# One transformer-and-retrieval encoder kernel on Trainium2: the routing table's transposes moved half a piece earlier, more table rounding on ScalarE, one key-score copy moved

## The reference

```python
q = (xc @ w_query).reshape(-1, PEER_HEADS, 2, PEER_HALF)
s1 = jnp.einsum('thd,hkd->thk', q[:, :, 0], sub_keys[:, 0]).astype(jnp.float32)
s2 = jnp.einsum('thd,hkd->thk', q[:, :, 1], sub_keys[:, 1]).astype(jnp.float32)
v1, i1 = lax.top_k(s1, PEER_TOPK)
v2, i2 = lax.top_k(s2, PEER_TOPK)
cand = (v1[..., :, None] + v2[..., None, :]).reshape(...)      # 256 sums per head
cidx = (i1[..., :, None] * PEER_N_KEYS + i2[..., None, :]).reshape(...)
sv, pos = lax.top_k(cand, PEER_TOPK)
eidx = jnp.take_along_axis(cidx, pos, axis=-1)
gate = jax.nn.softmax(sv, axis=-1)
u = u_tab[eidx]
act = jax.nn.gelu(jnp.einsum('thkd,td->thk', u, xc), approximate=False)
w = gate.astype(act.dtype) * act
return jnp.einsum('thk,thkd->td', w, v_tab[eidx])
```

## Time and profile before

| | us |
|---|---|
| median of 3 runs | 3840.44 (3839.34 to 3841.6) |
| the profiled execution | 3837.75 |
| its span in the trace | 3835.9 |
| PE busy | 3751.9 (98%) |
| ACT busy | 799.2 (21%) |
| POOL busy | 2339.5 (61%) |
| DVE busy | 2280.8 (59%) |

### The profile page before, as it was taken

How to read it: one execution, slowest core, us unless ns; L and a number is a source line. 1 busy time by engine, 2 the same in 40 slices (tenths; PEclk the granted TensorE clock), 3 DMA queues, 4 the chain that set the end, 5 groups by cost and what they waited for, 6 DMA issues and landing times.

```text
span 3835.9 us, 52905 instructions
## 1 busy us (share of the span) xinstructions
PE 3751.9 (98%) x18640; PEld 3098.6 (81%) x18640; DVE 2280.8 (59%) x3843; ACT 799.2 (21%) x1357; POOL 2339.5 (61%) x1204
## 2 busy tenths in 40 slices
PE   7999999999999999999999999999999999999998
PEld 6778887888888888888877788878888888888886
DVE  8545998994777422222385469989757773222224
ACT  1551112451111101111015411134411111101011
POOL 6445576336777666666664555853377776666664
PEclk9999999999999999999999999999999999999999
DMA  3122234887555333333222222358865553333331
GB/s 143 66 72 99 97 143 157 244 246 251 190 187 206 132 121 117 125 120 120 88 94 73 77 98 102 136 178 245 248 234 207 186 191 119 129 120 120 120 116 70
DMA packets 230075, 554.96 MB, mean 145 GB/s; under 512 B 10048, under 2 KB 141376, under 8 KB 181440
## 3 DMA queue, kind: packets, MB, share of 16 engines
q1 hardware_dynamic: 47680, 335.57, 24.6%
q10 hardware_dynamic: 182272, 217.75, 17.1%
HBM read 446.32 MB, written 106.95 MB: 144 GB/s over the span
## 4 chain that ended last, share of the span: by engine, by line
PE 91%; DVE 4%; POOL 2%; issue 2%; ACT 1%; DMA 0%; ACTq 0%; POOLq 0%; SPq 0%; DVEq 0%
PE bank L1161 28%; PE bank L1162 28%; PE bank L1163 28%; PE bank L1489 2%; PE bank L1490 2%; POOL part_l L405 1%; POOL part_h L416 1%; PE bank L1287 1%; PE bank L1447 1%; PE bank L1275 1%; DVE q_turn L844 0%; PE bank L1266 0%; PE bank L1267 0%; DVE tables L816 0%; DVE X L775 0%
## 5 line engine op out<-in xcount | busy, mean ns | idle before, releaser
L405 POOL TENSOR_TENSOR part_l<-landing,part_h 128x1024 fp32r<-128x1024 f32 x632 | 1636.5, 2592 | 372.5 <-ACT part_h L670 325.0
L416 POOL TENSOR_SCALAR part_h<-landing 128x1024 fp32r<-128x1024 f32 x564 | 706.8, 1253 | 1078.1 <-PE bank L1163 830.5
L1161 PE MATMUL bank<-XTh,part_h 128*128 128x512 f32 (+1 forms) x2688 | 1050.9, 391 | 18.3 <-POOL part_l L405 8.2
L1162 PE MATMUL bank<-XTl,part_h 128*128 128x512 f32 (+1 forms) x2688 | 1036.5, 386 | 0.0
L1163 PE MATMUL bank<-XTh,part_l 128*128 128x512 f32 (+1 forms) x2688 | 1036.5, 386 | 0.0
L1161 PE MATMUL bank<-part_h,Wh 128*128 128x512 f32 x2048 | 796.9, 389 | 0.9 <-POOL part_l L405 0.9
L1162 PE MATMUL bank<-part_l,Wh 128*128 128x512 f32 x2048 | 796.7, 389 | 0.0
L1163 PE MATMUL bank<-part_h,Wl 128*128 128x512 f32 x2048 | 796.7, 389 | 0.0
L1110 DVE TENSOR_TENSOR X<-X,bank 128x512 f32<-128x512 f32 x480 | 307.8, 683 | 549.8 <-PE bank L1163 549.8
L1161 PEld LDWEIGHTS bank<-XTh,part_h 128*128 128x128 f32 x2688 | 507.5, 189 | 120.7 <-issue 8.0
L1163 PEld LDWEIGHTS bank<-XTh,part_l 128*128 128x128 f32 x2688 | 507.1, 189 | 101.9
(11 more groups left out here) (172 smaller groups left out, 3396.6 us busy)
## 6 DMA issues: line engine op xcount, KB each, us to landing
landing<-stream SPq DMA_DIRECT2D x316, 1024.0 KB, 4.8
dense_gates<-spill ACTq DMA_DIRECT2D x32, 2048.0 KB, 9.3
gate<-dense_gates ACTq DMA_DIRECT2D x64, 1024.0 KB, 4.8
early_acts<-early ACTq DMA_DIRECT2D x144, 256.0 KB, 2.3
acts_in<-early_acts ACTq DMA_DIRECT2D x36, 1024.0 KB, 7.5
LNP<-ln ACTq DMA_DIRECT2D x5, 1024.0 KB, 4.7
X<-x SPq DMA_DIRECT2D x4, 512.0 KB, 9.5
keyT<-keys ACTq DMA_DIRECT2D x2, 1024.0 KB, 4.7
```

Source lines behind the costliest of these rows:

```text
L405: nc.gpsimd.tensor_tensor(part_l[s][:, w], landing[s][:, w], part_h[s][:, w].bitcast(F32), ALU.subtract).then_inc(split.sem, 1)
L416: nc.gpsimd.tensor_scalar(part_h[s][:, w], landing[s][:, w], 1.0, 0.0, ALU.mult, ALU.add).then_inc(high_part.sem, 1)
L1161: nc.tensor.matmul(dst, sth, mvh, start=first, stop=False)
L1162: nc.tensor.matmul(dst, sth, mvl, start=False, stop=False)
```

## The change

Four edits, in one layer's code and so in both layers. (1) `A_FIRST` goes from stream piece 48 to 34 and `A_PIECES` from 16 to 30: ScalarE now rounds `part_h` for table pieces 4 to 33, POOL for the others. (2) `high_ahead` counts pieces instead of quarters, and ScalarE calls it after each early piece from the third on, two pieces ahead. (3) The copy of the last head's key scores stands behind piece 1's Gelus instead of piece 0's. (4) The transposes of `route` stand ahead of piece 15 instead of between its halves, on TensorE and on ScalarE.

```diff
-A_FIRST, A_PIECES = P_TAB + E_BEFORE + 2, E_WITHIN
+A_FIRST, A_PIECES = P_TAB + 4, E_BEFORE - 2 + E_WITHIN
...
+                def high_ahead(b, n):
+
+                    s = n % SPLITS
+                    act.wait_ge(landed[s], l * (8 * NP) + b * 16 + ((P_TAB + n) // 2 * 16 + 16))
+                    act.wait_ge(used.sem, used.at(l, 2 * b + (P_TAB + n - SPLITS + 1)))
+                    for h in range(2):
+                        w = slice(h * PIECE // 2, (h + 1) * PIECE // 2)
+                        nc.scalar.copy(part_h[s][:, w], landing[s][:, w]).then_inc(high_within.sem, 1)
+
...
                     early_piece(i, 0, True)
-                    if i == 0:
+                    if i >= A_FIRST - P_TAB - 2:
+                        high_ahead(0, i + 2)
+                    if i == 1:
                         ks_copy(RH - 1)
-                early_piece(E_BEFORE - 1, 0, True, [0])
                 for tb in range(TB):
                     act.wait_ge(route_turned.sem, route_turned.at(l, tb + 1))
...
-                early_piece(E_BEFORE - 1, 0, True, [1])
+                early_piece(E_BEFORE - 1, 0, True)
+                high_ahead(0, E_BEFORE + 1)
...
                             if q == 7:
-                                high_ahead(b, 2 * k + 1)
+                                high_ahead(b, E_BEFORE + 2 + k)
...
                 pe.wait_ge(ks_copied.sem, ks_copied.at(l, RH))
-                for j in range(KD):
-                    early_product(E_BEFORE - 1, 0, j, True)
                 for tb in range(TB):
                     pe.wait_ge(routed.sem, routed.at(l, tb + 1))
...
-                for j in range(KD, 2 * KD):
+                for j in range(2 * KD):
                     early_product(E_BEFORE - 1, 0, j, True)
```

More of the change, by code:

```diff
@@ L661, in gate_block @@
                                       ).then_inc(spilled[k].sem, 16)
[L663 to L670, removed]
                 def early_half(b, c):
```

## The result

| | before | changed |
|---|---|---|
| median of the runs, us | 3840.74 | 3813.03 (3811.92 to 3815.32, 4 runs) |
| the profiled execution | 3837.75 | 3815.32 |
| its span | 3835.9 | 3813.5 |

The ratio is 0.993, 95% interval [0.9918, 0.9943]. The forecast was 3816.0 in 3811 to 3825. Repeated with the experiments, the same kernel gave 3813.12 (3809.22 to 3814.51) against 3840.07 for the kernel before (12 runs), 0.9927 [0.9913, 0.9941].

A forecast was written before the change was run, and what follows sets the result against it. TensorE, 91% of the chain, was taken as the bound. Per layer 1.91 + 2.1 + 7.42 = 11.4, or 12.6 by the stretch; 12.2 taken, 24.4 for two layers, giving 3816.0 us, range 3811 to 3825.

The forecast's parts named there:

- three small places: TensorE's waits after head 7's key scores (1.67 us), for `part_l` near pieces 12 to 14 (2.1), at one-hot rows (0.90, 4.53).
- The key-score copy: After head 7's key scores: piece 1's Gelus no longer queue behind the copy, giving back 1.91 us a layer.
- The whole sum: Per layer: 11.4 from listed waits, or 12.6 from the stretch 164.66 against 152.1 without a stop; 12.2 taken.
- together 7.42: At the first one-hot rows: earlier transposes remove stops of 0.90 and 4.53 and the slow restart of 1.99 us.
- The wait for POOL: TensorE's wait for `part_l` near pieces 12 to 14 goes as ScalarE takes the rounding: 2.1 us a layer.
- Is the table ready?: Before the transposes: `routed`, at 607.6 in the kernel before, must come by 606.5; expected at about 604.
- the 525.5 of the forecast's sums: Start of VectorE's first routing-table cycle in the sum for a partly late table, which ended at 615.9.
- POOL is silent: Around the exponential, until about 527, POOL waits for ScalarE, so VectorE's operations run free, some 4 us.
- The other estimate: For the table's end: if blocking of VectorE only shrank with POOL's load, `routed` would come at about 599.
- The one-hot rows: After the transposes: rows ready at 616.3 to 624.0, wanted by TensorE at 618.9 to 630.1; none late.
- Piece 8: Rival, chance 0.18: its rounding, behind the exponential, comes 1.3 to 3.4 us late a layer; time 3818.6 to 3822.8.
- The late table: Rivals at the transposes: table partly late, 9.4 us, 3834.8 (chance 0.12); late throughout, 17.3 us, 3854.6 (0.03).

The follow-up runs named there:

- key_only: The kernel before with only the last head's key-score copy moved behind piece 1's Gelus; median 3833.97 us, ratio 0.9985.
- turn_sooner: The changed kernel with the transposes a further half piece ahead, between piece 14's halves; median 3816.56 us, ratio 0.9939.
- turn_only: The kernel before with only the transposes of the routing table moved ahead of piece 15; median 3827.27 us, ratio 0.9967.
- exp_later: The changed kernel with the exponential of the picked sums placed after piece 6 instead of piece 5; median 3814.91 us, ratio 0.9936.

## Why the prediction was right, point by point

- **The bound and the places.** Right: all three small places of the earlier trace rows held the whole gain, in both layers.
- **The key-score copy.** Forecast 1.91, measured 1.98 when it is undone.
- **The whole sum.** Forecast 12.2 a layer, between the listed terms (11.4) and the stretch (12.6). The stretch was exact, 152.10 against 152.1. The 1.2 us that separate the two ways do come back once the stops are gone: in the kernel before 0.8 of them lie around the `part_l` waits and 0.3 beside the two stops at the rows. I should have taken the stretch, and the forecast would have been 3815.2. The measured median is 2 us lower still, which no trace explains.
- **The division of it.** This step failed. "So 0.90 + 4.53 come back ... together 7.42" was put under the transposes, and 2.1 under the rounding. Alone the transposes give 6.0 and leave a stop of 1.73, alone the rounding gives 7.5; undone they cost 3.1 and 4.9. I read the stop as VectorE starting late, which it was, and did not ask what stretched its second row. These rows of the kernel before, first POOL and then VectorE, show it, and I had not put them into the sum:

```profile
624.04 1.56 POOL L416 TENSOR_SCALAR part_h<-landing 128x1024 fp32r<-128x1024 f32 x1 [5.22 <-issue]
625.68 2.71 POOL L405 TENSOR_TENSOR part_l<-landing,part_h 128x1024 fp32r<-128x1024 f32 x1
628.37 1.48 POOL L416 TENSOR_SCALAR part_h<-landing 128x1024 fp32r<-128x1024 f32 x1
629.93 2.65 POOL L405 TENSOR_TENSOR part_l<-landing,part_h 128x1024 fp32r<-128x1024 f32 x1
```

```profile
626.06 2.88 DVE L1065 TENSOR_TENSOR hot<-iota,idx 128x1024 f16<-128x1024 f16 x1
628.98 1.41 DVE L1068 TENSOR_TENSOR hot2h<-hot,wth 128x1024 f16<-128x1024 f16 x1
630.31 2.82 DVE L1069 TENSOR_TENSOR hot2l<-hot,wtl 128x1024 f16<-128x1024 f16 x1
```

  The total was safe from this, since both edits were in the change; a forecast of one edit alone would have missed by 1.4 or by 5.4 a layer.
- **The wait for POOL.** Forecast some 4 us less in all, measured 12.7 - 8.4 = 4.3. With what matmuls lose around it the roundings of pieces 4 to 15 are worth 2.9 to 3.1 a layer, against the 2.1 in the sum.
- **Is the table ready?** Forecast `routed` at 604 and the transposes at 606.5. Less the 2.70 of the later start, the table was ready at 602.62 + 3.57 - 2.70 = 603.5 and the transposes began at 606.62. The number held in part by luck. Right was that the last cycles of 10.9 fall in step with the pieces. Not foreseen was the key copy: without the stop on the Gelu all of this comes earlier, the exponential by 1.9 (519.86 for 521.74), and the copy alone moves the start of the last step, the normalisation, 1.8 nearer to the key scores (125.69 for 127.47, key_only), more than the 1.1 that was needed. The first cycle so began at 521.86, 3.6 before the 525.5 of the forecast's sums, but the cycles were longer than forecast, and the normalisation began at 599.9, where by the 5.9 of the forecast's sums it would have begun at 598.1; it then took 3.57 instead of 5.9. "POOL is silent" is true, until 527.91 - 2.70 = 525.2, but "some 4 us" from it are not seen at the end of the table. The other estimate, 599 from POOL's smaller load, would have needed blocking to shrink with load. By the rule of the Trainium skill, page "SBUF — State Buffer", section "Who interferes with whom", that the prediction weighed, the moved roundings touch nobody: ScalarE's take 1.05 at the median in the changed kernel as before, and POOL's subtractions still hold VectorE as before (4.40 against 2.29 when free). The traces agree on both.
- **The one-hot rows.** Forecast: the first operation at 613.8, rows ready at 616.3, 618.9, 621.4 and 624.0, no row late. Measured, less 2.70: the first operation at 614.6, rows ready at 617.2, 619.7, 624.5 and 629.2. `part_l` blocks the third and the fourth once each, as worked out (the third's `hot2l` takes 2.89, the fourth's first operation 2.88). TensorE, at 3.74 a pair, never waits, but it takes the fourth at 630.1, so 0.9 is left of the 6.1 that the forecast had there before blocks.
- **The rivals.** None came. Piece 8 was not late: ScalarE's two roundings for it end at 526.78 + 2.00 = 528.8, POOL's pair for it ends at 533.8 and, at 2.35 or more for the second half, the first was done by 531.4, while TensorE comes to it at 530.4 + 2.7 = 533.1 and does not wait. The late table shows only where the transposes are moved further (turn_sooner).

## What to carry to other kernels

Price a stall by the stretch around it, from one fixed point to the next at which all variants run in step again: a sum of listed waits misses what matmuls lose beside each stop (1.2 of 12.6 here). Before a stop is credited to an edit, read what the late producer itself was doing: if it ran slow because another engine held it off, an earlier start and a lighter neighbour remove the same stop, and their gains don't add (6.0 + 7.5 gave 10.6). And when a producer falls in step with the consumer's pieces, don't count a head start before following it to the end: here leads of 2.0 and 3.9 us were both gone at the last step, whose start moved only with the pieces themselves (1.8).

## What the runs showed of the hardware

Three things. VectorE and POOL, both with operations ready, alternate one for one: VectorE's 0.68 us operations then take 1.41 to 2.88, POOL's 2.40 take 2.69 to 2.71 and its 1.06 take 1.34 to 1.49, over a whole row (turn_only). And VectorE's chain of three 2.29 us operations fell into the period of the pieces from two different starts: 2 us apart at the second cycle (changed and exp_later), they are 0.06 apart at the third. And a TensorE that had stood 4.53 us ran its next matmuls at a granted clock of 0.50 for about 4 us, while one that had stood 1.73 us ran on at 1.00 (before and turn_only).
